# Input-projection weights of a two-layer diffusion backbone: strided casting DMAs issued from GpSimd in the place of staged loads and cast copies

## What is computed

```
def _layer(x, mod, norm_g, w_in, ...):
    shift, scl, gate = jnp.split(mod, 3, axis=-1)
    xn = _rmsnorm(x, norm_g) * (1 + scl) + shift
    proj = xn @ w_in                       # 1024 x 2816, f32 in HBM
    q, k, v, z_a, h_c, b_c, c_c, z_c, u_p, z_p = jnp.split(proj, SPLIT_IDX, axis=-1)
    ...
    attn = _attend(q, k_all, v_all) * jax.nn.silu(z_a)
    out = jnp.concatenate([attn, conv, pool], axis=-1) @ w_out
    return x + gate * out, k, v
mod = jax.nn.silu(c) @ w_ada[l] + b_ada[l]   # per layer, 1024 x 3072
```

## Time and profile before

| | |
|---|---|
| median of 2 runs | 1734.61 us (1733.78 to 1735.44) |
| the profiled execution | 1744.64 us |
| its span on the slowest core (7) | 1743.1 us |
| spans of the cores | 1717.3 to 1743.1 us |
| busy: PE, ACT, DVE, POOL | 1210.7, 802.8, 605.2, 295.7 us |
| bytes moved by DMA on core 7 | 131.94 MB, mean 76 GB/s |
| loads of w_in | 96 (64 of 512 KB, 32 of 384 KB), all on SP's queue |
| POOL copies of w_in | 196 (28 of each of 7 lines), and 28 on DVE |

### The profile page before, as it was taken

The page is one execution under the profiler, slowest core; times in us unless marked ns, Lnnn a source line. Parts: engine busy times, 40 slices in busy tenths (PEclk is TensorE's granted clock), DMA queues, the critical chain, the costliest instruction groups (busy, mean ns, idle before and its releaser), DMA issues.

```text
span 1743.1 us, 17813 instructions; the slowest of 8 cores (1717.3 to 1743.1 us)
## 1 busy us (share of the span) xinstructions
PE 1210.7 (69%) x5342; PEld 476.3 (27%) x5342; DVE 605.2 (35%) x802; ACT 802.8 (46%) x1119; POOL 295.7 (17%) x372
## 2 busy tenths in 40 slices
PE   3645755547242477888788888888845788778986
PEld 0111122223121333233323332333223332233322
DVE  1121034224132434325333533432343443243232
ACT  0012033233631443874487368637814428742673
POOL 0100005442414012001201200134131120012000
PEclk9777977678565779999999999989976889977887
DMA  7752573740636010010001000116331100120001
GB/s 227 267 198 82 190 247 86 205 132 1 187 127 211 24 37 1 9 31 10 1 13 37 1 1 17 33 33 173 90 83 39 37 1 7 30 74 1 6 13 67
DMA packets 42798, 131.94 MB, mean 76 GB/s; under 512 B 5320, under 2 KB 10568, under 8 KB 40652
## 3 DMA queue, kind: packets, MB, share of 16 engines
q1 hardware_dynamic: 24792, 101.41, 18.8%
q10 hardware_dynamic: 17912, 29.39, 5.5%
HBM read 115.03 MB, written 7.36 MB: 70 GB/s over the span
## 4 chain that ended last, share of the span: by engine, by line
PE 40%; ACT 22%; DMA 13%; issue 8%; DVE 8%; POOL 6%; ACTq 2%; SPq 1%; DVEq 0%; POOLq 0%
ACT ptb L809 12%; PE pp L433 12%; PE pp L873 6%; PE pp L821 5%; DMA stg<-w_in 4%; DMA tD<-tB 4%; PE pp L802 3%; PE pp L800 3%; PE pp L823 3%; ACT ybf L380 3%; DMA stg<-w_out 2%; PE pp L271 2%; DMA xb<-w_ada 2%; PE pp L408 2%; PE pp L836 2%
## 5 line engine op out<-in xcount | busy, mean ns | idle before, releaser
L809 ACT ACTIVATE ptb<-pp 128x1024 bf16<-128x1024 f32 (+1 forms) x464 | 445.4, 993 | 144.9 <-PE pp L802 122.8
L433 PE MATMUL pp<-xn,wi 128*128 128x512 bf16 x1360 | 337.4, 411 | 52.8 <-ACT xn L415 38.3
L821 PE MATMUL pp<-ptb,Vst 128*128 128x512 bf16 (+1 forms) x464 | 178.5, 385 | 143.8 <-ACT ptb L809 142.9
L433 PEld LDWEIGHTS pp<-xn,wi 128*128 128x128 bf16 x1360 | 139.1, 104 | 237.6 <-issue 116.2
L800 PE MATMUL pp<-qT,KT 128*128 128x512 bf16 (+1 forms) x464 | 182.2, 393 | 4.3 <-DVE mix L733 3.2
L802 PE MATMUL pp<-qT,KT 128*128 128x512 bf16 (+1 forms) x464 | 182.4, 393 | 0.0
L823 PE MATMUL pp<-ptb,Vst 128*128 128x512 bf16 (+1 forms) x464 | 180.6, 389 | 0.0
L271 PE MATMUL pp<-xb,scs 128*2 128x512 f32 x192 | 104.3, 703 | 74.6 <-DMA xb<-w_ada 60.3
L873 PE MATMUL pp<-wo,mix 128*128 128x512 bf16 x512 | 129.1, 411 | 31.9 <-DVE mix L776 29.9
L821 PEld LDWEIGHTS pp<-ptb,Vst 128*128 128x128 bf16 x464 | 45.4, 98 | 331.6 <-issue 327.9
L752 DVE RECIPROCAL tB<-pp 64x512 f32<-64x512 f32 x18 | 60.5, 3360 | 146.6 <-PE pp L823 146.5
(11 more groups left out here) (176 smaller groups left out, 1294.9 us busy)
## 6 DMA issues: line engine op xcount, KB each, us to landing
stg<-w_in SPq DMA_DIRECT2D x64, 512.0 KB, 4.6
xb<-w_ada SPq DMA_DIRECT2D x16, 1536.0 KB, 8.2
stg<-w_in SPq DMA_DIRECT2D x32, 384.0 KB, 3.4
stg<-w_out SPq DMA_DIRECT2D x32, 256.0 KB, 4.7
stg<-w_out SPq DMA_DIRECT2D x16, 512.0 KB, 3.8
xb<-xs SPq DMA_DIRECT2D x4, 2048.0 KB, 13.7
tD<-tB ACTq DMA_DIRECT2D x48, 128.0 KB, 2.3
ys<-xb ACTq DMA_DIRECT2D x8, 512.0 KB, 2.7
```

The source lines that it names most:

```text
L433: last = e.matmul(banks[b][:, 0:nq], lhsT=wi[:, k, col0:col0 + 128], rhs=xn[:, k, 0:nq], start=(k == 0), stop=(k == 7))
L809: s.op("act", lambda e: e.activation(out=ptb[:, sl:sl + 2, 0:nq], in_=pp[st][:].rearrange("p (b n) -> p b n", b=2)[:, :, 0:nq], func=AF.Ex ...
L821: e.matmul(banks[po][:, 0:nq], lhsT=Vst[:, kts[2 * p][1], lo:lo + 128], rhs=ptb[:, sl, 0:nq], start=(p == 0), stop=False)
```

## The change

`prep_wi` is rewritten. It issues 35 DMAs on POOL's queue, which read f32 from HBM and write bf16 into `wi`, with no stage and no copy. One brings columns 512 to 767 of all row blocks. Then for each k come four, each of 128 partitions by 4 pieces of 64 columns: t=0 and t=1 of q, and t=0 and t=1 of z_a. Two more bring columns 1280 to 2047 and 2048 to 2815 of all row blocks. All have the stream name `wic`. In `program()` the first call stands in front of the whole `mod_layer(0)`, where it was interleaved with it; and the three `make_stats` of latent tokens stand behind the prompt's last `out_proj`, where they stood in front of the attention.

```
-        def prep_wi(l, ce="pool"):
+        def prep_wi(l, ce=None):
+            wsrc = win_d[l].rearrange("(k p) c -> p k c", p=128)
+            s.dma("pool", lambda e: e.dma_start(out=wi[:, :, 512:768], in_=wsrc[:, :, 512:768]), "wic", writes=WIR)
             for k in range(8):
...
-                sl = stage_slot()
-                s.dma("sp", lambda e, l=l, rows=rows, sl=sl: e.dma_start(out=stg[:, sl, :], in_=win_d[l, rows, 0:1024]),
-                      "stg%d" % sl, writes=["stg%da" % sl, "stg%db" % sl])
                 qv = wi[:, k, 0:512].rearrange("p (j t d) -> p j t d", j=4, t=2)
                 zv = wi[:, k, ZAO:ZAO + 512].rearrange("p (j t d) -> p j t d", j=4, t=2)
...
-                s.op(ce, c0, reads=["stg%da" % sl, "stg%db" % sl], writes=["wi%d" % k])
...
+                for t in range(2):
+                    s.dma("pool", lambda e, rows=rows, qv=qv, t=t: e.dma_start(
+                        out=qv[:, :, t, :], in_=win_d[l, rows, t * 256:(t + 1) * 256].rearrange("p (j d) -> p j d", j=4)),
+                        "wic", writes=["wi%d" % k])
+                for t in range(2):
+                    s.dma("pool", lambda e, rows=rows, zv=zv, t=t: e.dma_start(
+                        out=zv[:, :, t, :], in_=win_d[l, rows, ZAO + t * 256:ZAO + (t + 1) * 256].rearrange("p (j d) -> p j d", j=4)),
+                        "wic", writes=["wi%d" % k])
+            s.dma("pool", lambda e: e.dma_start(out=wi[:, :, 1280:2048], in_=wsrc[:, :, 1280:2048]), "wic", writes=WIR)
+            s.dma("pool", lambda e: e.dma_start(out=wi[:, :, 2048:2816], in_=wsrc[:, :, 2048:2816]), "wic", writes=WIR)
...
             load_x(xp_d, 0, 3)
-            mod_begin(0)
-            for k in range(8):
-                mod_chunk(0, k)
-                prep_wi_k(0, k, "dve" if k % 2 == 0 else "pool")
-            mod_end(0)
+            prep_wi(0)
+            mod_layer(0)
...
                 else:
                     prep_wi(0, "pool")
-                    for g in range(3):
-                        make_stats([4 * g + i for i in range(4)], 0, 0)
...
                 out_proj(PT, final=(l == 1), out_d=yp_d, row0=0)
+                if l == 1:
+                    for g in range(3):
+                        make_stats([4 * g + i for i in range(4)], 0, 0)
```

More of the change, by code:

```diff
@@ L311, in stage_slot @@
             return sl
-        def prep_wi(l, ce="pool"):
+        def prep_wi(l, ce=None):
+            wsrc = win_d[l].rearrange("(k p) c -> p k c", p=128)
+            s.dma("pool", lambda e: e.dma_start(out=wi[:, :, 512:768], in_=wsrc[:, :, 512:768]), "wic", writes=WIR)
             for k in range(8):
-                prep_wi_k(l, k, ce)
-        def prep_wi_k(l, k, ce="pool"):
-            if True:
                 rows = slice(k * 128, (k + 1) * 128)
-                sl = stage_slot()
-                s.dma("sp", lambda e, l=l, rows=rows, sl=sl: e.dma_start(out=stg[:, sl, :], in_=win_d[l, rows, 0:1024]),
-                      "stg%d" % sl, writes=["stg%da" % sl, "stg%db" % sl])
@@ L323, in prep_wi_k @@
                 qv = wi[:, k, 0:512].rearrange("p (j t d) -> p j t d", j=4, t=2)
                 zv = wi[:, k, ZAO:ZAO + 512].rearrange("p (j t d) -> p j t d", j=4, t=2)
-                def c0(e, k=k, sl=sl, qv=qv, zv=zv):
-                    e.tensor_copy(out=qv[:, :, 0, :], in_=stg[:, sl, 0:256].rearrange("p (j d) -> p j d", j=4))
-                    e.tensor_copy(out=qv[:, :, 1, :], in_=stg[:, sl, 256:512].rearrange("p (j d) -> p j d", j=4))
-                    e.tensor_copy(out=wi[:, k, 512:768], in_=stg[:, sl, 512:768])
-                    return e.tensor_copy(out=zv[:, :, 0, :], in_=stg[:, sl, 768:1024].rearrange("p (j d) -> p j d", j=4))
@@ L331, in prep_wi_k @@
-                s.op(ce, c0, reads=["stg%da" % sl, "stg%db" % sl], writes=["wi%d" % k])
-                sl = stage_slot()
-                s.dma("sp", lambda e, l=l, rows=rows, sl=sl: e.dma_start(out=stg[:, sl, :], in_=win_d[l, rows, 1024:2048]),
-                      "stg%d" % sl, writes=["stg%da" % sl, "stg%db" % sl])
-                def c1(e, k=k, sl=sl, zv=zv):
-                    e.tensor_copy(out=zv[:, :, 1, :], in_=stg[:, sl, 0:256].rearrange("p (j d) -> p j d", j=4))
-                    return e.tensor_copy(out=wi[:, k, 1280:2048], in_=stg[:, sl, 256:1024])
@@ L339, in prep_wi_k @@
-                s.op(ce, c1, reads=["stg%da" % sl, "stg%db" % sl], writes=["wi%d" % k])
-                sl = stage_slot()
-                s.dma("sp", lambda e, l=l, rows=rows, sl=sl: e.dma_start(out=stg[:, sl, 0:768], in_=win_d[l, rows, 2048:2816]),
-                      "stg%d" % sl, writes=["stg%da" % sl, "stg%db" % sl])
-                s.op(ce, lambda e, k=k, sl=sl: e.tensor_copy(out=wi[:, k, 2048:2816], in_=stg[:, sl, 0:768]),
-                     reads=["stg%da" % sl, "stg%db" % sl], writes=["wi%d" % k])
+                for t in range(2):
+                    s.dma("pool", lambda e, rows=rows, qv=qv, t=t: e.dma_start(
+                        out=qv[:, :, t, :], in_=win_d[l, rows, t * 256:(t + 1) * 256].rearrange("p (j d) -> p j d", j=4)),
+                        "wic", writes=["wi%d" % k])
```

## The result

The changed kernel takes 1849.06 us (median of 9 runs), the kernel before 1736.85 us beside it (8 runs): a ratio of 1.0646, with an interval of 1.0625 to 1.0667. It is 112 us slower; 1888 was forecast, within 1700 to 2080.

A forecast was written before the change was run, and what follows sets the result against it. No engine alone was taken to bound it; what counts is when `wi` is complete at its four uses. Terms 32 + 59 + 41 + 22 = 153 on 1744.6 gave 1897.7, less 10.0: 1888 us, range 1700 to 2080.

The forecast's parts named there:

- T: Length of one new filling of `wi`, first DMA to last landing: 140 us forecast, ends 83 and 213, against 63 before.
- the faster rival: POOL's small DMAs nearly as cheap as quiet SP or ACT ones, T below 84: -37, 1697 us; chance 0.10.
- Start: First filling, beside the first modulation: K projection at max(105, T + 25), 165 instead of 132.75 us, +32.
- the contention: First filling: delay of POOL's DMAs by w_ada and prompt loads, half of 48 us, 25 (0 to 48).
- Layer 0 to 1: Second filling, in the prompt: K projection waits for `wi`, T - 81.4, +59 us.
- Prompt to latent: Third filling: `prep_wo` behind `prep_wi` on POOL delays the first product with rope, T - 99.3, +41 us.
- latent 0 to 1: Fourth filling: the first product with rope comes at 1337 against 1315.33 us, T - 118.5, not below 0, +22.
- issued or landed: Last two fillings: POOL's `prep_wo` would start right when the last DMA is issued or landed; no size of its own.
- Costed at nothing: Effects given no term: SP's dropped w_in issues, POOL's dropped copies of 28 us per filling, earlier `stg` loads, lower clock.
- The clock: PE's clock, lower after longer waits (0.50 and 0.60 in the stretches), adds a few us at most.
- No change: Rival: T between 84 and 108, an awaited DMA about 2.4 us; at T = 100 +12, 1746 us; chance 0.15.
- Much slower: Rival: short runs, not waits, set the time; T = 213, +446, 2180 us; chance 0.10 for T above 188.

## Why the prediction was right

**The mechanism and the place.** 27 of 35 DMAs wait for the one before, and `wi` becomes the last thing that PE waits for at three of its four uses: as forecast, with DMA as the releaser and PE idle for 75.52, 60.62 and 46.21 us. The run without those waits turns +6.5% into -1.1%.

**T was somewhat too long.** Forecast 5.5 + 102 + 32.8 = 140. The second filling, core 0: 6.4 until the first small DMA is issued, 92.0 for the 32 small ones (327.25 to 419.28), 29.7 for the two big ones: 128. Of the 10 us that the small ones are shorter, 7 are in those that are not awaited, 0.73 instead of 1.5, and 3 in the awaited, 3.5 on the mean (3.1 to 3.3, and up to 3.8 behind one that is not awaited) instead of 3.75. In both POOL's part was mis-sized, 0.74 and not 1.5; its product over 128x512 at 1.16 was no measure for that. The count was one off: line 328 waits for the last small one too, so 25 are awaited and 7 are not, where the sum has 24 and 8, which is 2 us. (And the faster rival's lowest sum at T = 83 is -40, 1694 us, not -42.) The big ones take 12.9 instead of 16.4: the pace of w_ada was too low a bound, 3 MB in 12.9 us are 238 KB per us, about what the first stretch of the earlier trace rows moves.

An estimate worked out from the Trainium skill (DMA: Bandwidth & Descriptors, Anatomy of one DMA) has a small one at 2.3 us. Here it lands 2.8 us after the start of its issue at the median, POOL's 0.74 included, and the next issue starts another 0.3 to 0.5 us later; T = 80 was not reached. Where page and measurement differ, the measurement decides.

**Start: +32 forecast, +39 measured, by two errors that cancel.** T was 16 too long on the mean and the contention 19 too small: 25 forecast (half of 48 us of other transfers), 44 measured. (The rest is POOL's first issue at 1.6, and the 130.5 of the mean in the place of core 7's 132.75.) Halving assumed that the two queues share at each moment; but a DMA that is awaited sits out whatever large load lies beside it, 25.25, 8.09 and 13.98 us at a time, and POOL issues nothing meanwhile. `xn` was ready at 101.5 as forecast (105).

**Layer 0 to 1: +59 forecast, +41 measured.** T - 81.4 with T = 124 is 43. Only T was off.

**Prompt to latent: +41 forecast, +24 measured; latent 0 to 1: +22 forecast, +4 measured.** Here a step failed: the formula let `prep_wo` start when `wi` is complete. It starts when POOL has issued its last DMA, since nothing in `prep_wo` reads `wi`; the last 3 MB land beside it. T has to be replaced by T - 14 in both terms. With the last issue at 642.55 the third place is 123.5 - 99.3 = 24; the fourth has 114.0 + 0.9 against 118.5, so its slack is not used up, and the sum is 0, where 4 were measured. T itself was nearly as forecast in the third filling, 137.7 (519.05 to 656.76): there nearly the whole miss is this step. The prediction listed "issued or landed" as a thing to be seen, and its sum took the dearer of the two.

**The sum.** The places add up to 108 us where 153 were forecast. That the time still fell within the range owes something to its width, 380 us, and to the errors at the start having opposite signs.

**Costed at nothing.** The clock: in the second and third filling the granted clock was 0.57 and 0.56 on the mean (core 0, 320 to 449 and 519 to 656 us) where it had been 0.60 and 0.50, and the distance from the K projection of layer 1 to the third filling, where PE works on its projections, stayed what it was (70.1 and 70.5 us on the mean). The move of `make_stats`: shown by the two runs on it.

**Rivals.** Faster needed a small DMA at 2.1 us or less; POOL's wait of 2.4 behind each issue alone excludes it. No change needed T below 108: the wait of 2.4 alone was within its condition of 2.4, and it failed by POOL's 0.74. Much slower needed each small DMA to be as slow as those beside other loads; that happened to some of the first filling only. Its short runs have 30 of the 112 us.

## What to carry to other kernels

Count the waits that a scheduler puts between DMAs which write different parts of one tile: each costs a full landing time, and a chain of small ones is nearly as long as its count, whatever its runs are (2.8 to 2.9 us a link for 128 runs, 3.1 to 3.3 for 512). A filling that leaves its queue early is finished for the queue when its last DMA is issued and for its readers when that has landed; take the one or the other by who waits. And a DMA that is awaited before the next can be issued suffers from its neighbours' large loads in full, one after another, while unawaited ones make the neighbours suffer.

## What the runs showed of the hardware that had not been expected

- 512 runs of 128 B cost a casting DMA 0.3 to 0.4 us more than 128 runs of 512 B, 0.21 of it POOL's issue, though their packets take 1.7 times the time on the DMA engines (525 and 305 us).
- With both queues full, their packets' times 50.1 and 49.2% of the engines', a chunk of w_ada takes 12.7 us, against 8.2 at the median of the changed kernel.
- With 30 DMAs issued back to back at the start POOL stood for 32.72 us (core 0; 44.09 at most), with no releaser that the trace shows; in the second filling it paused after 23 of them, for 3.42 us (core 4), until one had landed. What sets that number stays open; it cost nothing that can be seen, since pacing the start moved the K projection by under 1 us.
- POOL's issue of a small DMA did not grow beside full engines: 0.74 us in the first filling as in the others.
- Keeping two row blocks or more in flight raises the landing time of the attention's 64 KB swaps (core 4) from 3.5 us in the kernel before to 4.2 (all 35) and 6.0 (two blocks), and the stretch from the second filling to the third takes 6 us more.
